# Memory attention and mLSTM in one pass over the heads behind the forgetting attention, key norms token-major, memory's softmax divided after its values

## The reference

```python
proj = rms_norm(x, norm_g) @ w_in
ya = spatial_gating(a_u, a_v, sgu_norm_g, sgu_w, sgu_b)
yb = forgetting_attention(b_q, b_k, b_v, b_f + fox_f_b, fox_q_g, fox_k_g)
yc = mlstm(c_qk, c_v, c_i + mlstm_i_b, c_f + mlstm_f_b, c_o, mlstm_conv_w, mlstm_conv_b, mlstm_out_g)
yd = rwkv7_time_mix(...)      # (token-shifted inputs)
ym = memory_attention(m_q, rms_norm(mem, mem_norm_g), mem_w_kv, mem_q_g, mem_k_g)
mixed = concatenate([y * silu(z) for y, z in ((ya, a_z), (yb, b_z), (yc, c_z), (yd, d_z), (ym, m_z))])
return x + mixed @ w_out

# memory attention: 512 queries against 256 memory rows, each head
s = einsum("bthd,bmhd->bhtm", rms_norm(q, q_g), rms_norm(k, k_g)) * HEAD_DIM ** -0.5
out = einsum("bhtm,bmhd->bthd", softmax(s, axis=-1), v)
# mLSTM, each head: a causal score times a decay weight; a numerator, and a denominator from the same weights
h = num / maximum(abs(den), exp(-m_t))
yc = rms_norm(sigmoid(o_logit) * h, out_g)
# rwkv, what is prepared for it
decay = exp(-exp(-softplus(-(w0 + tanh(w_lo) @ w2)) - 0.5))
a = sigmoid(a0 + a_lo @ a2)
kk = k * k_k / maximum(norm(k * k_k, per head), 1e-12)
```

## Time and profile before

| | |
|---|---|
| median of three runs | 1655.68 us (1654.29 to 1656.25) |
| time of the profiled execution | 1655.76 us |
| its span in the trace | 1654.0 us |
| PE busy, of the span | 1545.2 us (93%) |
| DVE / ACT / POOL busy | 681.1 / 532.0 / 552.2 us |
| DMA, mean over the span | 74 GB/s |
| 1303 to 1350 us (forgetting attention): PE busy | 43.16 of 47 us |
| 1350 to 1460 us (memory, mLSTM): PE busy | 81.72 of 110 us |

### The profile page before, as it was taken

How to read it: one execution, slowest core, us unless ns; L and a number is a source line. 1 busy time by engine, 2 the same in 40 slices (tenths; PEclk the granted TensorE clock), 3 DMA queues, 4 the chain that set the end, 5 groups by cost and what they waited for, 6 DMA issues and landing times. The chain is left out here.

```text
span 1654.0 us, 23421 instructions
## 1 busy us (share of the span) xinstructions
PE 1545.2 (93%) x9945; PEld 1325.3 (80%) x9945; DVE 681.1 (41%) x1345; ACT 532.0 (32%) x861; POOL 552.2 (33%) x215
## 2 busy tenths in 40 slices
PE   6999999999999999979998998999999987958998
PEld 6898885998988977758887997899798763647897
DVE  4032440322153443885545017332261343678424
ACT  3354225332123223233434112452433335131210
POOL 5324320332432349634632332333433100512021
PEclk9999999999999999989999999999999987568999
DMA  5222320224222232320101432342323000020111
GB/s 157 77 77 80 99 71 6 77 77 176 92 98 74 79 96 77 93 86 26 52 26 52 166 101 65 103 152 62 102 77 102 26 1 1 0 77 1 52 52 52
DMA packets 115970, 121.60 MB, mean 74 GB/s; under 512 B 14623, under 2 KB 109833, under 8 KB 115610
## 3 DMA queue, kind: packets, MB, share of 16 engines
q1 hardware_dynamic: 112320, 114.16, 22.0%
q10 hardware_dynamic: 3546, 5.94, 1.0%
HBM read 113.80 MB, written 6.29 MB: 73 GB/s over the span
## 5 line engine op out<-in xcount | busy, mean ns | idle before, releaser
L193 POOL TENSOR_TENSOR w_low<-w_ring,w_high 128x2048 fp32r<-128x2048 f32 (+1 forms) x92 | 419.9, 4564 | 815.2 <-ACT w_high L184 815.0
L209 PE MATMUL ps<-w_high,xT_high 128*128 128x256 f32 (+1 forms) x1056 | 304.3, 288 | 7.8 <-POOL w_low L193 3.4
L209 PE MATMUL ps<-w_high,xT_low 128*128 128x256 f32 (+1 forms) x1056 | 299.0, 283 | 0.0
L209 PE MATMUL ps<-w_low,xT_high 128*128 128x256 f32 (+1 forms) x1056 | 298.9, 283 | 0.0
L184 ACT ACTIVATE w_high<-w_ring 128x2048 fp32r<-128x2048 f32 (+1 forms) x92 | 173.7, 1890 | 303.6 <-PE ps L209 299.0
L209 PE MATMUL ps<-xT_high,w_high 128*128 128x512 f32 (+2 forms) x608 | 244.0, 401 | 1.0 <-ACT v_tok L636 0.7
L209 PE MATMUL ps<-xT_high,w_low 128*128 128x512 f32 (+2 forms) x608 | 240.4, 395 | 0.0
L209 PE MATMUL ps<-xT_low,w_high 128*128 128x512 f32 (+2 forms) x608 | 240.0, 395 | 0.0
L209 PEld LDWEIGHTS ps<-w_high,xT_high 128*128 128x128 f32 x1056 | 202.5, 192 | 15.5 <-POOL w_low L193 8.2
L209 PEld LDWEIGHTS ps<-w_low,xT_high 128*128 128x128 f32 x1056 | 202.5, 192 | 1.7 <-issue 1.7
L209 PEld LDWEIGHTS ps<-w_high,xT_low 128*128 128x128 f32 x1056 | 202.2, 191 | 0.0
(11 more groups left out here) (500 smaller groups left out, 2330.8 us busy)
## 6 DMA issues: line engine op xcount, KB each, us to landing
w_ring<-in_gla_w_in_dram SPq DMA_DIRECT2D x24, 1024.0 KB, 5.5
w_ring<-in_dsa_w_in_dram SPq DMA_DIRECT2D x19, 1024.0 KB, 5.2
w_ring<-in_w_in_dram SPq DMA_DIRECT2D x18, 1024.0 KB, 5.2
w_ring<-in_gla_w_out_dram SPq DMA_DIRECT2D x8, 1024.0 KB, 4.9
w_ring<-in_ple_gate_w_dram SPq DMA_DIRECT2D x8, 1024.0 KB, 5.1
w_ring<-in_dsa_w_out_dram SPq DMA_DIRECT2D x8, 1024.0 KB, 5.1
x_scratch<-x SPq DMA_DIRECT2D x4, 1024.0 KB, 6.8
w_ring<-in_w_out_dram SPq DMA_DIRECT2D x4, 768.0 KB, 4.8
```

The source lines that it names most:

```text
L193: self.nc.gpsimd.tensor_tensor(self.slot(self.w_low, i % RING, k, cols), self.slot(self.w_ring, n % RING, k, cols), self.slot(self.w_high, ...
L209: return self.nc.tensor.matmul(out, lhs, rhs, start=first, stop=last, skip_group_check=not check)
```

## The change

- **Barriers.** Those behind the forgetting attention and behind memory attention are gone. `phase_mem` and `phase_mlstm` become `phase_branches`, in the same block as the phase before, with waits on counts of its semaphores (`fox[...]`, `projected[...]`).
- **One pass over heads.** PE's order for head h is: turn memory's probabilities (8), logits of h+1, scores 0 and 1 of h+1, numerators of h, spread of h+2, memory values of h, scores 2 and 3 of h+1. Banks: spread 0, scores 1 and 2 (three before), numerators 3 (one head), logits 4 and 5, turned probabilities 6 and 7, memory's output 6.
- **Memory attention.** The probabilities aren't divided; the output is, by `mem_out`, 128 x 4 x 64 a head. The values are now 8 products of 128 x 64 (token-major), which adds eight transposes and a gate (`to_gated(..., "mem_y")`) at the end, and removes the four gates of 64 x 512.
- **mLSTM.** Absolute values, maximum, inverse, divide and sigmoid(o) go head by head (`divided`), so do squares and their sums. The output gain becomes a scalar of the gate instruction (`mlstm_out_g` as a column; one small transfer replaced by one in the column table). The turns of the gate rows, running maximum, `floor` and `pick` move into the projection (tile positions 34 to 37, which shift five later positions by one), as do tanh and silu of rwkv's z.
- **kk norms.** Squares (ACT) and the product with k_k (POOL) move to the start of the forgetting attention. The sums become token-major: 8 products of 128 x 2, then maximum, root and inverse on 128 x 16, four transposes to 4 rows, one copy, and two products of 4 x 512 that spread the inverse to all partitions, one DVE multiplication behind each.
- **Decay and gate.** Their four low-rank products and sigmoids move to the end of the forgetting attention.

The core of the diff:

```diff
-        gatings, gate_steps, gated_turns, gates_out = 37, 39, 41, 43
-        mem_turns = 44
+        a_turns, a_rows, mu_turns, mu_copies = 34, 35, 36, 37
+        gatings, gate_steps, gated_turns, gates_out = 38, 40, 42, 44
...
+                    pe.wait_ge(sem["kk_sq"], past["kk_sq"] + PAIRS)
+                    pe.wait_ge(sem["mem_kv_copied"], past["mem_kv_copied"] + 1)
+                    for j in range(NT):
+                        for i in range(PAIRS):
+                            ins = g.product(ps[:, 6, j * GH + 2 * i:j * GH + 2 * i + 2], s.kk_norm[:, i, j * P:(j + 1) * P], g.same64[:, 0:P:HD])
+                    ins.then_inc(sem["kk_sums"], add("kk_sums", 1))
...
+                    pe.wait_ge(sem["kk_rstd"], past["kk_rstd"] + 1)
+                    for j in range(NT):
+                        ins = nc.tensor.transpose(ps[0:GH, 6, j * P:(j + 1) * P], s.kk_tok[:, j * GH:(j + 1) * GH], g.ident[:])
...
+                def key_spread(i):
+
+                    if i == 0:
+                        pe.wait_ge(sem["kk_row"], past["kk_row"] + 1)
+                    else:
+                        pe.wait_ge(sem["kk_unit"], past["kk_unit"] + i)
+                    g.product(ps[:, 6, :], s.pair_of[:, i, :], s.a_row).then_inc(sem["kk_spread"], add("kk_spread", 1))
...
+                    if h == 1:
+                        key_sums()
...
                 memory_product(7)
+                pe.wait_ge(*projected["low_tanh"])
+                pe.wait_ge(*projected["low_rank_landed"])
+                pe.wait_ge(sem["fox_masked"], past["fox_masked"] + NT * GH)
+                key_spread(0)
+                low_product(0, 0, W_ROWS)
+                low_product(1, 1, W_ROWS)
+                key_spread(1)
+                pe.wait_ge(sem["kk_unit"], past["kk_unit"] + PAIRS)
+                low_product(0, 6, A_ROWS)
                 pe.wait_ge(sem["fox_scaled"], past["fox_scaled"] + GH)
                 to_gated(g, pe, y, [2, 3])
+                pe.wait_ge(sem["mem_kv_copied"], past["mem_kv_copied"] + 2)
+                low_product(1, 7, A_ROWS)
...
+                for n, (dst, i, bank, bias) in enumerate(((s.decay, 0, 0, "w0"), (s.decay, 1, 1, "w0"), (s.a_gate, 0, 6, "a0"), (s.a_gate, 1, 7, "a0"))):
+                    act.wait_ge(sem["low_in"], past["low_in"] + n + 1)
+                    nc.scalar.activation(dst[:, i, :], ps[:, bank, :], ACT.Sigmoid, bias=g.col(bias)[:, i:i + 1]).then_inc(sem["low_sigmoid"], add("low_sigmoid", 1))
...
-
-def phase_mem(g, s):
+
+def phase_branches(g, s):
...
                 def spread(h):
 
+                    if h == 0:
+                        pe.wait_ge(*fox["low_sigmoid"])
+                        pe.wait_ge(*projected["pick"])
+                    else:
+                        pe.wait_ge(sem["weight_log"], past["weight_log"] + NT * h)
+                    g.product(ps[:, SPREAD, :], s.pick[:, h, :], s.mu_row).then_inc(sem["mu_spread"], add("mu_spread", 1))
...
+                def mem_values(h):
+
+                    pe.wait_ge(sem["mem_probT"], past["mem_probT"] + MT * (h + 1))
+                    for j in range(NT):
+                        for i in range(MT):
+                            ins = g.product(ps[:, OUT, j * HD:(j + 1) * HD], probT[:, i, j * P:(j + 1) * P], s.mem_kv[:, i, GW + h * HD:GW + (h + 1) * HD], i == 0, i == MT - 1)
+                    ins.then_inc(sem["mem_o"], add("mem_o", 1))
...
                 for h in range(GH):
+                    mem_turn(h, 0)
+                    mem_turn(h, 1)
+                    if h + 1 < GH:
+                        mem_logits(h + 1)
+                        scores(h + 1, (0, 1))
+                    numerators(h)
                     if h + 2 < GH:
                         spread(h + 2)
+                    mem_values(h)
                     if h + 1 < GH:
-                        products(h + 1)
+                        scores(h + 1, (2, 3))
+                pe.wait_ge(sem["mem_scaled_out"], past["mem_scaled_out"] + GH)
+                to_gated(g, pe, y_mem, [4, 5], "mem_y")
+                pe.wait_ge(sem["mlstm_scaled"], past["mlstm_scaled"] + 1)
+                to_gated(g, pe, y, [1, 2], "mlstm_y")
...
+                def mem_out(h):
+                    rows = slice(h * NT, (h + 1) * NT)
+                    dve.wait_ge(sem["mem_exp"], past["mem_exp"] + NT * (h + 1))
+                    nc.vector.reciprocal(inv[:, rows], total[:, rows]).then_inc(sem["mem_inv"], add("mem_inv", 1))
+                    dve.wait_ge(sem["mem_inv"], past["mem_inv"] + h + 1)
+                    dve.wait_ge(sem["mem_o"], past["mem_o"] + h + 1)
+                    nc.vector.tensor_tensor(head(y_mem, h), ps[:, OUT, 0:NT * HD].rearrange("p (j d) -> p j d", j=NT), inv[:, rows].unsqueeze(2).to_broadcast([P, NT, HD]),
+                                            ALU.mult).then_inc(sem["mem_scaled_out"], add("mem_scaled_out", 1))
+
+                def divided(h):
+                    dve.wait_ge(sem["den_abs"], past["den_abs"] + h + 1)
+                    nc.vector.tensor_tensor(den[:, :, h], den[:, :, h], s.floor[:, :, h], ALU.max).then_inc(sem["den"], add("den", 1))
+                    dve.wait_ge(sem["den"], past["den"] + 2 * h + 1)
+                    nc.vector.reciprocal(den[:, :, h], den[:, :, h]).then_inc(sem["den"], add("den", 1))
+                    dve.wait_ge(sem["den"], past["den"] + 2 * h + 2)
+                    num = ps[:, NUM, 0:NT * W].rearrange("p (j w) -> p j w", j=NT)[:, :, 0:HD]
+                    nc.vector.tensor_tensor(head(y, h), num, den[:, :, h].unsqueeze(2).to_broadcast([P, NT, HD]), ALU.mult).then_inc(sem["mlstm_y"], add("mlstm_y", 1))
+                    dve.wait_ge(sem["mlstm_y"], past["mlstm_y"] + h + 1)
+                    nc.vector.tensor_tensor(head(y, h), head(y, h), head(s.o_sig, h), ALU.mult).then_inc(sem["mlstm_o"], add("mlstm_o", 1))
+
...
+                for h in range(GH):
+                    if h + 1 < GH:
+                        peaks(h + 1)
+                        weighted(h + 1, (0, 1))
+                    if h + 2 < GH:
+                        logs(h + 2)
+                    mem_out(h)
+                    divided(h)
+                    if h + 1 < GH:
+                        weighted(h + 1, (2, 3))
+                    if h == 0:
+                        decay_before()
+                    if h:
+                        square_sums(h - 1)
```

More of the change, by code:

```diff
@@ L1873, in _ @@
                     src = ps[:, i % NB, :]
+                    if i == low_tanh:
+                        act.wait_ge(sem["projected_by_dve"], past["projected_by_dve"] + nth_of[("small", 0)])
+                        nc.scalar.activation(s.low[W_ROWS, :], s.low[W_ROWS, :], ACT.Tanh).then_inc(sem["low_tanh"], add("low_tanh", 1))
                     if i == conv_silus:
@@ L2433, in phase_mem @@
-    g.sem.end_phase()
-def phase_mlstm(g, s):
-    nc, t, ps = g.nc, g.t, g.ps
-    sem, past, count, add = g.sem, g.sem.past, g.sem.count, g.sem.add
-    PAIRS = GH // 2
-    with ExitStack() as stack:
-        a_row, mu_row = g.room[0:GH, 2, 4, :], g.room[0:GH, 2, 5, :]
-        pick = g.room[0:GH, 2, 6, :].rearrange("p (h t) -> p h t", h=GH)
-        mu = g.sb(stack, "mu", [P, NT, GH])
-        floor = g.sb(stack, "floor", [P, NT, GH])
+        prob = g.sb(stack, "mem_prob", [P, 2, NT, N_MEM])
@@ new lines, in numerators @@
+                def numerators(h):
+                    if h:
+                        pe.wait_ge(sem["mlstm_y"], past["mlstm_y"] + h)
+                    pe.wait_ge(sem["weighted"], past["weighted"] + NT * (h + 1))
+                    for j in range(NT):
+                        for i in range(j + 1):
+                            ins = g.product(ps[:, NUM, j * W:(j + 1) * W], score[:, h % 2, i, j * P:(j + 1) * P], s.vC[:, i, h, :], i == 0, i == j, check=False)
+                    ins.then_inc(sem["mlstm_num"], add("mlstm_num", 1))
@@ L2517, in _, with weights @@
[L2517 to L2522 removed]
+                def weights(h):
@@ new lines, in squares @@
+                def squares(h):
+                    act.wait_ge(sem["mlstm_o"], past["mlstm_o"] + h + 1)
+                    nc.scalar.activation(head(sq, h), head(y, h), ACT.Square).then_inc(sem["mlstm_sq"], add("mlstm_sq", 1))
+                weights(0)
+                mem_exps(0)
+                for h in range(GH):
+                    if h + 1 < GH:
+                        weights(h + 1)
+                    mem_copies(h)
+                    if h + 1 < GH:
+                        mem_exps(h + 1)
+                    denominators(h)
+                    if h == 2:
+                        act.wait_ge(sem["before"], past["before"] + 1)
+                        nc.scalar.activation(s.decay[:], s.decay[:], ACT.Exp, scale=-DECAY_SCALE).then_inc(sem["decays"], add("decays", 1))
+                        nc.scalar.activation(s.decay_at[:], s.log_decay[:], ACT.Exp, scale=-DECAY_SCALE).then_inc(sem["decays"], add("decays", 1))
```

(26 more changed lines are left out.)

444 lines of the change are left out of this document (204 added, 240 removed).

## The result

The changed kernel is slightly slower: 1660.33 us median of 20 runs (1655.24 to 1663.88) against 1656.29 (1654.29 to 1662.53); the ratio is 1.0022 (95% interval 1.0016 to 1.0029). Forecast were 1652 us and a gain. The profiled execution took 1662.07 us (span 1660.3); it lies in the upper part of the runs, so its difference to the one before (6.3 us) holds some 2 us that the medians (4.0) don't.

The account below looks back on a forecast made before the run. PE was taken to set the pace, with 28.3 us of waits and a low clock behind 1350 us. Terms +0.7, -4.6 and +0.5 summed to -3.4, from 1655.68 to a forecast of 1652 us, range 1638 to 1661.

Parts of the forecast that it names:

- The projection: Projection stage: eight added small transposes on a full PE cost 0.6 to 1.1 us, taken as +0.7.
- Inside the forgetting attention: Forgetting attention: key sums and four transposes add 2.2 us on PE's path, plus 0.8 for handovers.
- rival 2: Forgetting attention: narrow key sums lower PE's clock; 3 to 5 us or up to 17 lost, 1656 to 1668; chance 0.17.
- The tail and prologue: Forgetting attention's end and mLSTM/memory start: tail 10.3 plus 0.8 for sigmoids; prologue 13.7 plus 2.0 of waiting.
- The heads: Common memory and mLSTM stage: 20.2 us for a full head at 1.2 GHz, 68.5 for all four, up to 1446.7.
- The cover: In the heads, PE work hides ACT's copies (2.03 us) and `mem_out` (0.42 on DVE).
- The end: From the last head's PE work to rwkv_prep: 8.7 us, so rwkv_prep starts at 1455.4 against 1460.0, -4.6.
- The sum: Whole kernel: +0.7 - 4.6, and +0.5 for unplaced handovers, gives -3.4 us.
- Rival 1: Heads: gapless PE work restores the clock, 11 to 12 us a head; about 1630, or 1641 half the time; chance 0.15.

Follow-up runs that it names:

- e1: Changed kernel with the gate row's and mu's transposes and copies one tile later in the projection; 1653.61 us, ratio 0.9984 to the kernel before.
- e11: The changed kernel run again unaltered; 1660.57 us, ratio 1.0019 to the kernel before.
- e3: As e1, with the eight narrow key sums of kk run twice (16 products); 1660.24 us, ratio 1.0026 to the kernel before.
- e4: As e1, with scores, memory's logits and spreads of mu on 128 rows, zeros added; 1613.62 us, ratio 0.9745 to the kernel before.
- e5: As e4, but the spread of mu stays a product on 4 rows; 1620.52 us, ratio 0.9791 to the kernel before.

## Why the prediction was wrong

**The projection, forecast +0.7, measured +9.9 in the profile (in e1 +4.4).** This is the step that failed: "were they late, `gatings` ... would hold PE for about one DVE instruction". I asked what waits behind the new turns, and not whether their own input is there when PE comes. It was to be read in the trace of before. PE was through with the last sums of the gates (tile 33) at 1205.8, and tile 34 takes 2.8 us:

```profile
1205.47 0.37 PE L209 MATMUL ps<-log_gates,not_before 128*128 128x8 f32 x2
```

DVE made a_tok at 1213.3, behind a long queue:

```profile
1202.97 1.22 DVE L1933 TENSOR_TENSOR heads<-heads,head_ss 128x1024 f32<-128x1024 f32 x1
...
1207.46 4.56 DVE L1933 TENSOR_TENSOR heads<-heads,head_ss 128x1024 f32<-128x1024 f32 x1
...
1213.29 0.17 DVE L1953 TENSOR_TENSOR a_tok<-gates,cum 128x16 f32<-128x16 f32 x1
```

1213.5 less 1208.6 is 4.9 us, the wait that was then measured as 4.7. Nobody waited for a_tok there before, so no row of waits named it.

The rest of the 9.9: 0.6 was already lost before 1150; 1.6 because the clock was 0.83 from 1160 to 1170, where it was 1.00 before, with PE busy throughout; the eight transposes 1.4, with what they hold up; and 2.3 for the other work at 1.2 GHz behind the pause (the clock fell at 1214.8, within the wait, and was back at 1221.2). Less 0.5 for a wait for `heads` that only the kernel before has, that makes 10.1. The 1.6 are not tied to the change: e1, with nearly the same list, has the same drop, and e11 and e3 don't.

**Inside the forgetting attention, forecast +3.0, measured +5.7.** The sums (1.84) and transposes (0.44) were right, as e1 shows (+2.3). The clock fell behind the sums in both profiles of the changed kernel; that was rival 2, to which I gave 0.17 with a decision at 4 us. Its mild form happened (3.4 us), in some executions; the clock was back before the tail, and the last memory product then ran at 1.95 instead of 3.57.

**The tail and prologue, forecast 11.1 and 15.7.** Measured 10.9 (1363.95 to 1374.88) and 15.7 (to 1390.58), of which 1.6 us is a wait for the weighting, where I had put 2.0. In the tail two errors offset each other. Its products and `to_gated` took 9.5 us where I had 10.3, because the first four products, two pairs, still ran at full clock, in 3.12 us (1.12 for each pair would be 2.24, one after another 4.48), and half clock came at 1368. Then the turns of memory's first inputs took 1.5, where I had 0.8 for the sigmoids.

**The heads, forecast 68.5 at 20.2 each.** Measured 68.1. Prices read at the same clock from the trace of before, added up as starts, held to 1%. The cover held too; `mem_out` shows 0.6 us at the very end only.

**The end, forecast 8.7.** From the end of the last values (1458.6) to rwkv_prep 8.8. (The forecast took 1460.0 for the old start of rwkv_prep where the rows have 1460.4, so its own terms give 3.8, not 3.4.)

**The sum.** With most of the wait removed (e1) the kernel is 0.16% (2.3 us in medians) faster than before, where I had forecast 3.4 to 4. So the common stage did what was forecast (8.5 us less from the tail to rwkv_prep), and the clock stayed low in the heads as forecast; the sign was turned mostly by a move of 1.4 us of work to a place whose input was 4.7 us late, with the clock's fall in that wait. That 1660.3 still lies inside the range of 1638 to 1661 is luck: the range reached so far up for rival 2, not for this wait.

**Rival 1** (0.15) needed more than a gapless list: with the list gapless the clock was 0.50. Its price for a head was too high by 1 to 2 us: I had 11 to 12, bound by DVE, and with full rows a head takes 10.0 to 10.3, with 0.5 us of waiting for DVE in one of them. The kernel goes to 1614 then, where I had put this case at 1630 and, with the clock up half of the time, at 1641.

## What to carry to other kernels

When an instruction is moved, look up in the trace when its input is made at the new place, even if nothing waits for that input today; a producer that is late for nobody shows in no list of waits. Read the granted clock as a price of its own: here, at 1.2 GHz, filling gaps gave 10 us of 1656, and making the same products run on all 128 rows with zeros gave 40. And do both: interleaving was worth three times as much once the clock was up, and full rows without it left PE waiting.

## What the runs showed of the hardware

- The granted clock was 0.50 over 68.00 busy of 68 us with scores and logits on 64 rows and spreads on 4, and 1.00 over 34.11 busy of 36 us with the same products on 128 rows, zeros included (e4); with the spreads alone on 4 rows it was 0.86 (e5).
- One DVE product of 128 x 1024 took 4.56 us where the same one took 1.22 (above); POOL ran its own of 128 x 2048 beside it, from 1206.31 to 1210.94:

```profile
1206.31 4.63 POOL L193 TENSOR_TENSOR w_low<-w_ring,w_high 128x2048 fp32r<-128x2048 f32 x1 [6.58 <-ACT w_high L184]
```

The Trainium skill (Trainium Architecture — The Big Picture, "What this means for kernel authors") has DVE and POOL share a port to SBUF under an exclusive lock. The trace agrees for this pair: the DVE product took 5.25 and 4.56 us in the two places where POOL was at its own, and ended 1.08 us behind POOL's end both times; with POOL idle it took 1.22. The same two are long, 4.50 to 5.26 us, in all 14 profiles. It doesn't hold for every pair: at 1415.77, beside POOL's products of 128 x 128, a DVE product of 128 x 1024 took 1.22. Of the 4.9 us by which a_tok is late, the second long product alone accounts for 3.3 (4.56 less 1.22, an estimate; no run takes POOL's product away).
- Executions of one instruction list differ by where the clock falls. Single runs of the changed kernel lie between 1653 and 1664 us; the clock from 1160 to 1170 was 0.83 in one of its profiles and 1.00 in the other.
